# Between two layers of a transformer kernel: the last expert's sum formed in PSUM, the normalisation moved into the transposes, and the copies cut in thirds

## What is computed

```python
for l in range(DEPTH):                                     # DEPTH = 2
    update_ctx = l < DEPTH - 1
    h  = modulate(rms_norm(x,  g_pre_a), sh_a,  sc_a)      # rows scaled by 1/rms, then per column * gain + shift
    hc = modulate(rms_norm(xc, g_pre_a), csh_a, csc_a)
    mix, mix_c = token_mixers(h, hc, ...)
    x = x + gt_a * rms_norm(mix @ w_out[l], g_post_a)      # and xc likewise if update_ctx
    h = modulate(rms_norm(x, g_pre_f), sh_f, sc_f)
    x = x + gt_f * rms_norm(expert_choice_ffn(h, ...), g_post_f)
    # with update_ctx: the same for xc
return x

def expert_choice_ffn(h, w_router, w_gate, w_up, w_down):
    cap = 2 * n // 16                                      # 64 of 512 latent rows, 32 of 256 context rows
    aff = softmax(h @ w_router)
    g, idx = top_k(aff.T, cap)                             # each expert picks its rows
    xs = h[idx]
    hid = silu(xs @ w_gate) * (xs @ w_up)
    y = (hid @ w_down) * g
    return zeros_like(h).at[idx].add(y)                    # the experts' rows are summed
```

## Time and profile before

| | us |
|---|---|
| median of 3 runs | 2186.5 |
| the profiled execution | 2191.71 |
| its span | 2189.9 |
| PE busy | 1920.4 (88%) |
| DVE busy | 544.8 (25%) |
| ACT busy | 472.3 (22%) |
| POOL busy | 162.7 (7%) |
| DMA, mean over the span | 247 GB/s |

### The profile page before, as it was taken

The page is one execution under the profiler, slowest core; times in us unless marked ns, Lnnn a source line. Parts: engine busy times, 40 slices in busy tenths (PEclk is TensorE's granted clock), DMA queues, the critical chain, the costliest instruction groups (busy, mean ns, idle before and its releaser), DMA issues.

```text
span 2189.9 us, 25241 instructions
## 1 busy us (share of the span) xinstructions
PE 1920.4 (88%) x10460; PEld 895.2 (41%) x10460; DVE 544.8 (25%) x1164; ACT 472.3 (22%) x967; POOL 162.7 (7%) x230
## 2 busy tenths in 40 slices
PE   5998998999849999999998299879993998988885
PEld 3655554775423333333333155446741333332331
DVE  1021452672250000000000402346615011111113
ACT  4131112442311011110111513114412111110111
POOL 0000010110110101101011000011101000000000
PEclk9999999999969999999999599989996999999997
DMA  9111149301369999999997412000017999999994
GB/s 390 39 54 62 39 204 426 139 11 58 129 266 359 395 395 388 391 394 394 396 376 309 161 39 77 0 10 30 11 58 312 404 427 428 429 427 429 428 427 186
DMA packets 52750, 541.77 MB, mean 247 GB/s; under 512 B 6352, under 2 KB 8656, under 8 KB 23232
## 3 DMA queue, kind: packets, MB, share of 16 engines
q1 hardware_dynamic: 34400, 486.72, 53.9%
q0 software_dynamic: 18128, 53.95, 7.5%
q10 hardware_dynamic: 144, 0.01, 0.0%
HBM read 516.54 MB, written 24.12 MB: 247 GB/s over the span
## 4 chain that ended last, share of the span: by engine, by line
PE 71%; DMA 18%; DVE 6%; ACT 3%; issue 1%; POOL 0%; SPq 0%; PEldq 0%; PEld 0%; DVEq 0%; POOLq 0%; ACTq 0%
DMA ring<-in_wstream 17%; PE ps L1658 15%; PE ps L1337 9%; PE ps L1721 7%; PE ps L1558 6%; PE ps L1666 5%; PE ps L1315 5%; PE ps L1728 3%; PE ps L1505 3%; PE ps L1443 2%; PE ps L1307 1%; PE ps L1478 1%; PE ps L1258 1%; PE ps L1285 1%; PE ps L1471 1%
## 5 line engine op out<-in xcount | busy, mean ns | idle before, releaser
L1658 PE MATMUL ps<-ring,work 128*64 128x512 f32 x2048 | 464.6, 606 | 37.0 <-DMA ring<-in_wstream 32.6
L1658 PEld LDWEIGHTS ps<-ring,work 128*64 128x64 f32 x2048 | 145.5, 139 | 349.9 <-issue 290.2
L1721 PE MATMUL ps<-big,work 128*64 128x512 f32 x1024 | 237.1, 605 | 3.1 <-ACT work L710 3.1
L1187 DVE TENSOR_TENSOR work<-glao,ps 128x512 f32<-128x512 f32 x32 | 22.0, 687 | 831.9 <-ACT glao L716 440.1
L1337 PE MATMUL ps<-hT,ring 128*128 128x512 f32 (+1 forms) x592 | 206.4, 507 | 1.9 <-DVE hT L856 1.4
L1337 PEld LDWEIGHTS ps<-hT,ring 128*128 128x128 f32 x592 | 112.2, 190 | 95.0 <-issue 86.4
L1558 PE MATMUL ps<-ring,hT 128*128 128x512 f32 x320 | 138.7, 592 | 0.0
L1721 PEld LDWEIGHTS ps<-big,work 128*64 128x64 f32 x1024 | 68.3, 138 | 140.3 <-issue 131.2
L1666 PE MATMUL ps<-ring,work 128*32 128x512 f32 x1024 | 119.8, 597 | 0.0
L1315 PE MATMUL ps<-ring,hT 128*128 128x384 f32 (+3 forms) x384 | 110.9, 450 | 0.0
L632 ACT ACTIVATE work<-ps,work 128x512 f32<-128x512 f32 (+2 forms) x120 | 81.9, 684 | 62.3 <-DVE work L996 31.5
(11 more groups left out here) (253 smaller groups left out, 2004.5 us busy)
## 6 DMA issues: line engine op xcount, KB each, us to landing
ring<-in_wstream SPq DMA_DIRECT2D x166, 2048.0 KB, 14.3
big<-in_wstream SPq DMA_DIRECT2D x64, 2048.0 KB, 13.3
x_kept<-big POOLq DMA_DIRECT2D x14, 512.0 KB, 2.9
big<-x_kept POOLq DMA_DIRECT2D x14, 512.0 KB, 6.8
xn_lat<-big POOLq DMA_DIRECT2D x8, 512.0 KB, 16.2
big<-in_x_all SPq DMA_DIRECT2D x6, 512.0 KB, 6.5
work<-in_nat_bias POOLq DMA_DIRECT2D x16, 192.0 KB, 2.7
big<-in_x_all POOLq DMA_DIRECT2D x6, 512.0 KB, 6.3
```

The costliest lines, as they stand in the source:

```text
L1658: last = T.matmul(bank(m)[64 * h:64 * h + 64, :], XST[:, kc, e, 0:CAP_L], gate_up[j][:, kk, m * D + h * 512:m * D + (h + 1) * 512], start= ...
L1721: last = T.matmul(bank(3)[64 * g:64 * g + 64, :], HT[:, kc, 0:CAP_L], down[j][:, kc % 4, h * 512:(h + 1) * 512], start=kc == 0, stop=kc == ...
```

## The change

1. **Last expert of layer 0.** Its rows no longer go to DRAM. After expert 14's add POOL reads the sums into XN, not ACC (`ACC_READ`). The last expert's down products are evacuated as before; DVE builds one-hot matrices for it (`ptok`). On PE `last_middle` first multiplies the context rows into banks 0 to 3 (four groups of 32 rows), DVE adds these to XN; for each latent tile the bank takes the identity times XN, and the expert's product on top. The results are read straight from the banks.
2. **Order of the transfers.** X is read back after the sums; its first four tiles wait for slot 4 alone. SP waits for all six before it asks for layer 1's first units.
3. **Post-processing of layer 0.** `post` is split in `post_att`, `post_ffn` (ACT), `post_middle` and `post_last` (DVE). In the middle POOL does the add to X (`x_next`), with two buffers `GAIN_X`. XN is not written any more: DVE makes a diagonal matrix of the tile's 1/rms (`NORM`, identity times a scalar, 128x128), and PE multiplies X by it, which transposes and scales at once.
4. **Copies by thirds.** The transposes come in three stages of two tiles (256 columns, all eight blocks of 128 rows in banks 4 to 7); the copies to `hT` go to ACT (stage 0), DVE (stage 1) and half to each (stage 2).
5. **Gain rows early.** The diagonals are built in `post_att` after the first tile, PE multiplies them in `route` between logits and affinities, ACT copies them to `GROW_F` after the Exp of the softmax. A Sqrt on a dummy column stands ahead of `post_ffn`.
6. **Experts of layer 0.** Latent down products go to bank 6 and the context transposes to bank 3; ACT evacuates the context part first, behind its own semaphore `down_ctx`, and waits for the adds of two experts back ahead of it.
7. **End of layer 1.** The last products are by whole tiles, two banks each, with one DVE add of 1024 columns; SP stores the output instead of POOL.

```diff
 (SP)
                 if l == 0:
+                    for t in tiles(l):
+                        sp.wait_ge(sem(f"x_rows{t}"), X_AGAIN[l])
                     for n in range(IN_AT[1], FFN_AT[1]):
...
+            for t in range(NLT):
+                sp.wait_ge(sem("x_ready"), t + 1 + (DEPTH - 1) * NLT)
+                sp.dma_start(out[t * P:(t + 1) * P, :], X[:, t, :]).then_inc(sem("stored"), 16)
 (POOL)
                 def x_again():
-                    for j in range(RING, SLOTS):
-                        pool.wait_ge(ffn_used[j], (l + 1) * NE)
-                    for t in tiles(l):
+                    for t in sorted(tiles(l)):
+                        if t in (0, NLT):
+                            pool.wait_ge(ffn_used[RING + t // NLT], (l + 1) * NE)
                         pool.dma_start(X[:, t, :], xkeep[t * P:(t + 1) * P, :]).then_inc(sem(f"x_rows{t}"), 16)
+                def x_next(i):
+                    t = tiles(l)[i]
+                    pool.wait_ge(sem("y_used"), i + 1 + before("y_used", l, "f"))
+                    pool.wait_ge(sem(f"x_rows{t}"), X_AGAIN[l])
+                    pool.tensor_tensor(X[:, t, :], X[:, t, :], GAIN_X[i % 2], ALU.add).then_inc(...)
...
-                        if i == PAIRS - 1:
-                            x_again()
-                        scatter_add(2 * i + 1)
-                    pool.wait_ge(sem("added"), ZERO_DMAS + 32 * NE)
+                        if i < PAIRS - 1:
+                            scatter_add(2 * i + 1)
+                    pool.wait_ge(sem("added"), ZERO_DMAS + 32 * (NE - 1))
...
-                        pool.dma_start(ACC[:, t, :], src).then_inc(sem(f"x_rows{t}"), 16)
+                        pool.dma_start(XN[:, t, :], src).then_inc(sem(f"x_rows{t}"), 16)
+                    for t in tiles(l):
+                        pool.wait_ge(sem(f"x_rows{t}"), ACC_READ)
+                    x_again()
+                    for i in range(NT):
+                        x_next(i)
 (ACT)
+            def post_ffn(l):
+                ts = tiles(l)
+                S.activation(AFM[:, 15:16], ones[:, 0:1], ACT.Sqrt)
...
+                    output_square(0)
+                    output_square(1)
+                    for i, t in enumerate(ts):
+                        if i + 2 < len(ts):
+                            output_square(i + 2)
+                        norm_square(l + 1, "a", i, t)
+                        if i == 2:
+                            act.wait_ge(sem("cols"), 4 * (l + 1) + 2)
+                            act.wait_ge(sem("xT"), 1 + before("xT", l + 1, "a"))
+                            h_next(range(KC), 0)
+                    act.wait_ge(sem("xT"), 3 + before("xT", l + 1, "a"))
+                    h_next(range(KC // 2, KC), 2)
...
                 S.activation(LOG[:, 0:nt, :], LOG[:, 0:nt, :], ACT.Exp).then_inc(sem("logit_exp"), 1)
+                gate_rows(l, "f")
...
-                    act.wait_ge(ffn_used[5], i * 2 + (e + 1 + l * NE))
                     if ctx_too:
                         n = 2 * i + e
                         if n >= 2:
                             act.wait_ge(sem("added"), ZERO_DMAS + 32 * (n - 1))
-                        S.activation(YL[e], bank(3), ACT.Copy, scale=VALT[:, n:n + 1])
-                        S.activation(YC[e][:, 0:D // 4], ...).then_inc(sem("yev"), 1)
+                        act.wait_ge(sem("down_ctx"), n + 1)
+                        out_ = S.activation(YC[e][:, 0:D // 4], ...)
+                        if n == NE - 1:
+                            out_.then_inc(sem("yev_ctx"), 1)
+                    act.wait_ge(ffn_used[5], i * 2 + (e + 1 + l * NE))
+                    if ctx_too:
+                        S.activation(YL[e], bank(6), ACT.Copy, scale=VALT[:, n:n + 1]).then_inc(sem("yev"), 1)
 (DVE, post_middle)
+                def gain(i):
+                    t = ts[i]
+                    dve.wait_ge(sem("psq"), i + 1 + before("psq", l, "f"))
+                    link(V.reciprocal(rs[:, t:t + 1], ss[:, t:t + 1]))
+                    if i == 2 or i == 3:
+                        dve.wait_ge(sem("xc_ready"), i - 1)
+                    elif i > 3:
+                        dve.wait_ge(sem("x_ready"), i - 3 + l * NLT)
+                    src = XN[:, t, :] if t >= NLT else ps[:, (t % 2) * D:(t % 2) * D + D]
+                    V.scalar_tensor_tensor(GAIN_X[i % 2], src, rs[:, t:t + 1], GROW_F[...], ALU.mult, ALU.mult)\
+                        .then_inc(sem("y_used"), 1)
+                def normal(i):
+                    t = ts[i]
+                    dve.wait_ge(sem("sq"), i + 1 + before("sq", l + 1, "a"))
+                    link(V.reciprocal(rs[:, NT + t:NT + t + 1], ss[:, NT + t:NT + t + 1]))
+                    V.tensor_scalar(NORM[:, t, :], ident, rs[:, NT + t:NT + t + 1], None, ALU.mult).then_inc(sem("xn"), 1)
+                for i in range(len(ts)):
+                    gain(i)
+                    if i:
+                        normal(i - 1)
+                    if i == 0:
+                        mod_cols(l + 1, 0)
+                dve.wait_ge(sem("xT"), 2 + before("xT", l + 1, "a"))
+                h_next(range(KC), 1)
+                normal(len(ts) - 1)
+                dve.wait_ge(sem("xT"), 3 + before("xT", l + 1, "a"))
+                h_next(range(KC // 2), 2)
 (PE, route)
                 last.then_inc(sem("logits"), 1)
+                gate_rows(l, "f")
                 pe.wait_ge(sem("aff"), 1 + l * PER["aff"])
 (PE, last_middle)
+                def whole(t):
+                    pe.wait_ge(sem(f"x_rows{t}"), ACC_READ)
+                    if t == 0:
+                        pe.wait_ge(sem("acc"), NCT)
+                    elif t >= 2:
+                        pe.wait_ge(sem("y_used"), NCT + t - 1 + before("y_used", l, "f"))
+                    for h in range(2):
+                        T.matmul(bank(2 * (t % 2) + h), ident, XN[:, t, h * 512:(h + 1) * 512], start=True, stop=False)
...
+                def turn_next(stage):
+                    ts = tiles(l)[2 * stage:2 * stage + 2]
+                    if stage == 1:
+                        pe.wait_ge(sem("h_ctx"), 1 + before("h_ctx", l + 1, "a"))
+                    elif stage == 2:
+                        pe.wait_ge(sem("h_t"), 1 + before("h_t", l + 1, "a"))
+                    for j, t in enumerate(ts):
+                        pe.wait_ge(sem("xn"), 2 * stage + j + 1 + before("xn", l + 1, "a"))
+                        for k in range(KC):
+                            last = T.matmul(ps[...], X[:, t, k * P:(k + 1) * P], NORM[:, t, :], start=True, stop=True)
+                    last.then_inc(sem("xT"), 1)
+                whole(0)
+                whole(1)
+                turn_next(0)
+                whole(2)
+                whole(3)
+                turn_next(1)
+                turn_next(2)
```

More of the change, by code:

```diff
@@ new lines, in post_att, with h_next @@
+                    dve.wait_ge(sem("y_used"), i + 1 + before("y_used", l, "a"))
+                    dve.wait_ge(sem(f"x_rows{t}"), X_BACK[l])
+                    V.tensor_tensor(X[:, t, :], X[:, t, :], GAIN_X[0], ALU.add).then_inc(sem("x_mid"), 1)
+                    dve.wait_ge(sem("x_mid"), i + 1 + l * PER["x_mid"])
+                    if i:
+                        rms(l, "f", i - 1, tiles(l)[i - 1])
+                rms(l, "f", i, t)
+            def h_next(ks, half):
+                for k in ks:
+                    src = ps[:, 2048 + k * 256:2048 + (k + 1) * 256]
+                    last = V.tensor_scalar(hTv[:, k, (half - 1) * 256:half * 256], src, colv[:, 0, 0, 0, k:k + 1], colv[:, 0, 0, 1, k:k + 1],
+                                           ALU.mult, ALU.add)
+                last.then_inc(sem("h_t"), 1)
@@ new lines, in post_last, with last_add @@
+            def post_last(l):
+                ts = tiles(l)
+                def last_add(i):
+                    t = ts[i]
+                    dve.wait_ge(sem("comb"), LAST_COMB + i + 1)
+                    c = 2 * (i % 2)
+                    V.tensor_tensor(ACC[:, t, :], ACC[:, t, :], ps[:, c * 512:c * 512 + D], ALU.add).then_inc(sem("acc"), 1)
+                last_add(0)
+                last_add(1)
+                for i, t in enumerate(ts):
+                    dve.wait_ge(sem("psq"), i + 1 + before("psq", l, "f"))
+                    link(V.reciprocal(rs[:, t:t + 1], ss[:, t:t + 1]))
+                    link(V.scalar_tensor_tensor(GAIN_X[0], ACC[:, t, :], rs[:, t:t + 1], GROW_F[:, 0:D], ALU.mult, ALU.mult))
+                    dve.wait_ge(sem(f"x_rows{t}"), X_AGAIN[l])
+                    V.tensor_tensor(X[:, t, :], X[:, t, :], GAIN_X[0], ALU.add).then_inc(sem("x_ready"), 1)
+                    dve.wait_ge(sem("x_ready"), t + 1 + l * NLT)
+                    if i + 2 < len(ts):
+                        last_add(i + 2)
@@ L1237, in _ @@
                 mod_cols(l, 1)
[L1238 removed]
+                post_att(l)
                 h_out(l, "f")
@@ L1758, in ffn @@
```

(17 more changed lines are left out.)

218 lines of the change are left out of this document (126 added, 92 removed).

## The result

| us | before | after |
|---|---|---|
| median of five runs each, on the same chip | 2189.61 (2184.46 to 2191.57) | 2166.54 (2160.48 to 2171.85) |
| the profiled execution | 2191.71 | 2162.2 |
| its span | 2189.9 | 2160.4 |
| PE busy | 1920.4 | 1931.2 |
| POOL busy | 162.7 | 172.1 |

The ratio is 0.9905, with a 95% interval of 0.9884 to 0.9926: about 21 us faster (16 to 25). The forecast was 2174.1, the range 2165 to 2182. It holds the time, near its lower end, and the sign is right. The terms of the sum are not all right, and one of them is missing.

A forecast was written before the change was run, and what follows sets the result against it. The prediction saw a fully exposed 60.4 us gap between the layers, with PE idle for over 40 us. It summed -13.9 (gap), +3.9 (routing) and -2.4 (end) to -12.4, so 2174.1 us, range 2165 to 2182.

The forecast's parts named there:

- The stretch between the layers: Last down product of layer 0 to layer 1's projection: gap of 60.4 us falls to 46.5, -13.9 us.
- The turn taken at 5.8: PE's turn of the last two tiles before the projection: 3.5 us at high clock, 7.0 at low, taken at 5.8.
- The 1.4 us for a cold clock at the start of the projection: Start of layer 1's projection: part may run at 1.2 GHz, costing up to 2 us, taken at 1.4.
- the step that said that the reads would have the DMA engines to themselves: Between the layers: SP loads layer 1's units only when X is back; tiles 4 and 5 there by about 1199.5.
- The port: Between the layers: DVE and POOL exclude each other; each diagonal waits for POOL's add (2.3 us, six times), second gain too.
- rival 1: Between the layers: no DVE-POOL exclusion, clock mostly up; -17 to -21 us in all, 2166 to 2169; chance 0.25.
- Rival 2: Between the layers: PE becomes the bound, at the low clock; 2179 to 2187 us; chance 0.14.
- The routing: Gain-row products on PE between logits and affinity transposes: +3.0 us in layer 0, +0.9 in layer 1, together +3.9.
- The end: End of layer 1: whole-tile products, one DVE add and an earlier table load bring the last add 2.4 us earlier.
- The stores: Output stores issued by SP instead of POOL at the end: taken as nothing, with -0.8 to +1.5 us.

The follow-up runs named there:

- m1: The kernel after with the six 128x128 diagonals made by ACT, DVE keeping the reciprocals: 2164.4 us, ratio 0.9889, stretch between the layers 44.7 us.
- m2: The kernel after with the add to X on DVE behind the gain product, POOL without arithmetic: 2162.26 us, ratio 0.9879, stretch between the layers 44.2 us.
- m3: The kernel after with SP asking for layer 1's weights at once, not waiting for X: 2178.14 us, ratio 0.9962, stretch between the layers 58.0 us.
- m4: The kernel after with PE's gain-row products of both layers moved behind the transposes of the affinities: 2161.15 us, ratio 0.9874.
- w3: w2 plus five idle PE products of 512 columns, three ahead of the last turn and two behind it: 2152.25 us, ratio 0.9855, stretch 38.0 us.
- w2: m4 with the first tile pair's eight copies moved to DVE and the second pair's split between ACT and DVE: 2157.05 us, ratio 0.9875, stretch 41.5 us.
- w1: m4 plus seven idle PE products of 512 columns, five ahead of the last turn and two behind it: 2160.15 us, ratio 0.989, stretch 45.4 us.
- t1: The kernel before with only the output stores moved from POOL to SP: 2176.63 us, ratio 0.9951.
- t2: The kernel after with the output stores given back to POOL: 2171.4 us, ratio 0.9928.
- t3: The kernel after, SP still storing, but POOL also waiting for the stores at its end: 2172.07 us, ratio 0.9933.
- t4: The kernel before with POOL storing the first three tiles and SP the last: 2182.45 us, ratio 0.998.

## Why the prediction was right, and where it was not

**The stretch between the layers.** The chain was the forecast one. From the last down product (1194.6 in the forecast, 1194.06 measured), forecast and measured: first gain done 5.0 and 5.4; POOL's second add done 11.1 and 11.8; diagonal of the second tile 15.4 and 15.8; ACT free for its copies 22.4 and 23.3; POOL's last add done 33.1 and 34.1; DVE's eight copies done 37.3 and 37.8; projection 45.1 and 45.4. The turn taken at 5.8 took 5.47. The 1.4 us for a cold clock at the start of the projection did not come (10.56, as before 10.57), which makes -15.0 of the -13.9; in m1, m2 and m3 the same 32 records took 12.26, so it was a fair term. Since m3 loses 12.6 us by SP's wait alone, the step that said that the reads would have the DMA engines to themselves had to hold for most of the gain. No run takes out the last expert's products, the diagonals or the thirds by themselves, so what each of these is worth stays open.

**The port.** Right in kind, and no longer on one thin row: 2.32 for 0.17, 2.40 for 0.29, and neither in m2, where POOL adds nothing. In count it was wrong: the forecast had each of the six diagonals wait for an add. Three did, each ending with one (0.57, 1.50 and 2.40); at the other three no add was running, and they took 0.29. The second gain was not drawn out either (1.28): the 128x8 copy ahead of it was, and held it back as long. These four waits are the ones that stand in the forecast chain, so its times come out all the same. The Trainium skill ("SBUF — State Buffer", section "Who interferes with whom") says that a DVE copy or tensor_scalar in a two-port mode, or one with two SBUF inputs, excludes a GpSimd instruction that reads SBUF, and that one with at most one SBUF input outside those modes doesn't. In which mode an instruction ran no trace says; otherwise the traces agree on both halves: the drawn-out instructions are copies and tensor_scalars from SBUF to SBUF and the gain product with two SBUF operands (3.05 in m1 and m4, 3.15 in w3), and the reciprocal (0.16 at 1205.18, beside POOL) and the copies from PSUM (3.71 for eight in w3) are not. It goes the other way round too: in w2 that gain product had begun at 1199.68, POOL's add at 1200.48, and it was the add that took longer, 2.69 for 2.35. The 4 to 7 us that rival 1 gave the exclusion were not tested: m2 has none, and its stretch is 1.2 us shorter, but it also does the adds on DVE. Counted from the last down product, ACT's eight copies are done at 26.1 for 27.3 and DVE's eight at 35.7 for 37.8, and a turn of 6.35 at a lower clock gives 0.9 back. What is queued on ACT counts either way: w2 moves its copies, and the stretch falls by 3.5.

**The clock.** Rival 2 (PE at the low level throughout) is out: the clock is 1.00 from 1205 to 1220, and low only in the first tile's products (0.59 from 1199 to 1202) and in the two turns of 32 records. The last turn, which the forecast had nearer to the low level because PE would have waited, came after a pause of 5.03 us and took 5.47; with products ahead of it (w1) 3.84.

**The routing.** Layer 0: forecast +3.0, measured +2.5, and m4 shows the cause. The products took 5.38, at a mean clock of 0.68 and between the 3.7 and 7 of the bounds. In m2 they ran at 1.00, took 3.68, and the stretch was 37.0, +0.8: so 1.7 of the 2.5 are the clock's. Layer 1: forecast +0.9, measured 0. I had taken the middle of 0.2 to 1.9, where the records (1.96 for four, had 1.98) and the idle time (1.66) left 0.3; the transposes of the affinities start 2.7 us after the logits in both kernels.

**The end.** -2.4 forecast and measured.

**The stores: the step that failed.** "I take nothing, with -0.8 to +1.5." They brought -8.3, as t1 shows alone and t2 by taking it back. I had priced the issue (0.28 and 0.53) and asked only what SP's would cost, and had not asked what fills the 11.3 us between the last add and the end of the span, of which issue and landing explain 3.2. With the store at -8.3 and the rest as forecast the sum would have been -20.7 and the forecast 2165.8; measured 2166.5.

So the range held partly by luck. The forecast's own range, 2170 to 2179, would have missed. The measured 2166.5 lies in the 2166 to 2169 of rival 1, whose mechanism is false: the time by itself would have seemed to prove that DVE and POOL don't exclude each other. t2, the change without its stores, is the test of what I had reasoned about: 15.7 us faster (12.0 to 19.2) against a forecast of 12.4.

## What to carry to other kernels

Read the end of the span like any other stretch: last issue plus landing against the span's end; if the engine that waits last there is POOL, try giving the last wait to another (8.3 us here). When transfers that someone waits for would stand behind large ones that no one needs yet, hold back the large ones: here the rest of the new stretch kept 2.4 of its 15.0 us without that (m3). Products that may hide under a search should stand behind what starts it, and in a chain that several engines hand on, moving the work queued ahead of a hand-over (the eight copies here: the stretch fell from 45.0 to 41.5 in w2) can be worth more than speeding up a step (the adds, 1.2 in m2).

## What the runs showed of the hardware

- A program whose last wait is POOL's ends 7.7 to 8.1 us after that wait is met (the kernel before, t2, t3, t4), whether POOL issued the DMA or not; with SP's it ends 0.4 us after (the kernel after, 2160.0 and 2160.4; t1, 2178.1 and 2178.5). Landings are taken from the median of the page.
- DVE's copy of 128x8 took 2.32 and its tensor_scalar of 128x128 2.40 when POOL's add of 128x1024 (2.35) had begun ahead of them, 0.17 and 0.29 alone. POOL's add took 2.34 to 2.36 wherever it began first, 2.42 (m4) behind a 128x8 copy and 2.69 (w2) behind a gain product with two SBUF operands.
- 32 turns of 128x128 took 3.8 us at the high level of PE's clock and 5.4 to 6.5 at lower means. After the same pause of 1.84 us the clock stayed at 1.00 in the kernel after and in w3; in w1 its mean was 0.71 from 1208 to 1211, in w2 0.99 there and 0.50 from 1211 to 1214.
